# The last heads of a fused two-block transformer kernel: values between logits and masks, queries and keys transposed later, outputs split earlier

## The chip, the cores and the metric

The kernel runs on one NeuronCore of a Trainium2 chip. The metric is the device time of one execution in microseconds. TensorE (PE in the profile) does matmuls and transposes; VectorE (DVE), ScalarE (ACT) and GpSimd (POOL) do the elementwise work; SyncE (SP) issues the loads of weights. Each engine runs a program of its own in order, and the programs meet at semaphores.

## The reference

Two transformer blocks on a sequence of 256 tokens of width 1024, in float32. The first has two attention branches of 8 heads, a merge and a gated extra input. The second has two layers, each with a token mixer, a cross-attention of 4 heads to a memory of 256 entries, an output projection and an MLP. The change touches the second layer of the second block, whose mixer is this attention of 12 heads (with 256 tokens there is a single block of keys, so only the causal part is left):

```python
q, k, v = jnp.split(qkv, 3, axis=-1)
q = apply_rope(rms_norm(heads(q), q_gain), cos, sin)
k = apply_rope(rms_norm(heads(k), k_gain), cos, sin)
s_own = jnp.einsum('bhcd,bhkd->bhck', qc, k_own).astype(jnp.float32) * scale
s_own = jnp.where(kpos[None, :] <= qpos[:, None], s_own, NEG_2)
p = jax.nn.softmax(s, axis=-1).astype(v.dtype)
out = jnp.einsum('bhck,bhkd->bhcd', p_own, v_own)
...
x = x + jnp.concatenate([tok, mo], axis=-1) @ w_out[i]
u = rms_norm(x, g_mlp[i])
x = x + jnp.square(jax.nn.relu(u @ w_ff1[i])) @ w_ff2[i]
```

## The kernel before

**Dense products.** Activations (transposed, `a_hi`, `a_lo`, `b_hi`, `b_lo`) and weights are each split into a high and a low part, and a product is three matmuls, hi*hi, hi*lo and lo*hi. Weights come in units of 128 x 2048. SyncE loads a unit into `raw` (two places), ScalarE writes `w_hi` from it, VectorE `w_lo` (`unit(u)` on either engine splits unit u+3, into a ring of four), and TensorE multiplies: 24 matmuls of 128 x 512 a unit (`product`, L1796). SyncE may load unit u once `w_lo` of u-2 is made.

**Heads.** Heads are worked in pairs, by steps. Step n brings the logits of pair n, while the pair n-1 has its probabilities transposed and the pair n-2 is multiplied with its values. Between these small pieces TensorE runs a *fill*, a dense product that has nothing to do with the heads (`fill_of`, `one_fill`). There are three runs of steps; the change touches the last, `RUN3`, pairs 14 to 21 and steps 14 to 23. Pairs 14 and 15 are memory heads (their queries see all 256 keys, so their second half of keys has twice the width), 16 to 21 are the 12 causal heads. The fills of steps 14 to 19 are a whole unit each of the projection that makes the queries, keys and values of later pairs; those of steps 20 to 23 are a quarter of a unit each, six matmuls, of the output projection.

**The pieces of a step on TensorE**: `logits(n)`, `masks(n)` (adds the causal mask by a matmul with the identity and raises `s_ready`; memory heads have none), `qk_parts(n+1)` (transposes queries and keys of the next pair into the bank `b_io`), `values(n-2)` (raises `pv_done`), `transposes(n-1)` (the probabilities; the first half of the keys goes into bank `b_t`, the second into `b_io` too), and the fill. In `last_step`, a step n with n+1 in `LATE_PARTS` runs `qk_parts(n+1)` as a `mid` of its fill, before the third of four k-tiles; the others run it right behind the masks. Since both use `b_io`, an early `qk_parts(n+1)` comes before `transposes(n-1)`, which waits for its copy; a late one comes after, and waits until VectorE has copied the second half of pair n-1 (`pt_cp_v`).

**The others.** In step n ScalarE does `copy_qk(n+1)` (early, or late, behind `copy_pt`), for some steps squares of the next heads' rows (`SQUARES_AT`, used in steps 16 and 18), `exps(n, (0,))`, `out_hi(n-2)` (the high part of the pair's output, into `b_hi`), `exps(n, (1,))`, `copy_pt(n-1)`, the normalisation of the second head, the split of a unit, and an eviction of a block. VectorE does `maxima(n)` (two reductions and a small operation into `nmx` for each of the two heads), reductions of the squares, `copy_pt(n-1)`, the softmax factors and the normalisation of the first head, `out_lo(n-2)` (L1416), the split of a unit, an eviction. GpSimd rotates and scales queries and keys (`norm_and_rotate`) and raises `moba_made`, for which `qk_parts` waits.

`values(n)` waits for the low part of the pair before it, since both pairs' outputs use one bank:

```python
pe.wait_ge(pt_cp_a, pr + 1)
pe.wait_ge(pt_cp_v, pr + 1)
if pr:
    pe.wait_ge(pair_lo, pr)
```

and `logits(n)` waits for the exponentials of the step before: `pe.wait_ge(exp_done, 2 * (n - 1) + (1 if n % 2 == 0 and n > N_IDX else 2))`.

Of the kernel before, what the change touches and what calls it, by code (L numbers as in the profile page):

```python
# [84 lines left out]
RUN1, RUN2, RUN3 = range(0, 12), range(12, 14), range(14, 22)  # L85
# [71 lines left out]
BR_FILL = {12: 0, 13: 1}  # L157
DRAIN = (12, 13, 22, 23)
MOBA_FILL = {14 + i: i for i in range(6)}
LATE_PARTS = (16, 18, 20)  # L160
OUT_FILL = {20: 0, 21: 1, 22: 2, 23: 3}

SQUARES_AT = {15: (("k1", B_MOBA + 1), ("q2", B_MOBA + 1)), 17: (("k2", B_MOBA + 2),)}
# [26 lines left out]
def build(nc, a, out):  # L190
    with ExitStack() as ctx:
# [532 lines left out]
        def _(act):  # L724
# [14 lines left out]
            def unit(u):  # L739

                v = u + LOOK
                if v < N_UNITS:
                    split(v, v % RING, land_slot(v), unit_size(v))
# [101 lines left out]
            def last_step(n):  # L845

                if n + 1 in RUN3 and n + 1 not in LATE_PARTS:
                    copy_qk(n + 1)
                for squares_ in SQUARES_AT.get(n - 1, ()):
                    head_squares(*squares_)  # L850
                exps(n, (0,))
                if n - 2 in RUN3:
                    out_hi(n - 2)
                exps(n, (1,))
                if n - 1 in RUN3:
                    copy_pt(n - 1)
                if n + 1 in LATE_PARTS:
                    copy_qk(n + 1)
                if n - 1 in SQUARES_AT:
                    normalise_second(n)  # L860
                for u, k, half_, ks in fill_of(n):
                    if 3 in ks and u < U_MOBA + 7:
                        unit(u)
                if n - 1 not in SQUARES_AT:
                    normalise_second(n)
                for u, k, half_, ks in fill_of(n):
                    if half_ and 3 in ks:
                        block_done(u)
                        evac(k)
                late_unit(n)  # L870
# [27 lines left out]
            def exps(n, heads=range(2)):  # L898

                pr = n - N_IDX  # L900
                if pr >= 2:
                    act.wait_ge(pt_ready, pr - 1)
                else:
                    act.wait_ge(idx_acc, n - 1)
                for h in heads:
                    act.wait_ge(max_done, 2 * pr + h + 1)
                    for t in range(NT):
                        factor = SCALE if pr < N_GATES else query_factor(n, h)[:, t:t + 1]
                        logits = logits_of(n)[:, h, t, 0:width0(n) if t == 0 else S]
                        ins = act.activation(prob_of(n, t)[:, h, :], logits, ACT.Exp, scale=factor,  # L910
                                             bias=nmx[:, pr, t, h:h + 1], accum_out=psums[:, pr, t, h:h + 1])
                    ins.then_inc(exp_done, 1)
# [11 lines left out]
            def out_hi(n):  # L924

                pr = n - N_IDX
                if pr < N_GATES:
                    act.wait_ge(pair_tmp, pr + 1)
                    act.activation(b_hi[:, pair_ktile(pr), :], gated[:], ACT.Copy).then_inc(pair_hi, 1)
                    return  # L930
                act.wait_ge(pv_done, pr + 1)
                act.activation(b_hi[:, pair_ktile(pr), :], out_of(n), ACT.Copy).then_inc(pair_hi, 1)
# [262 lines left out]
        def _(dve):  # L1195
# [165 lines left out]
            def maxima(n):  # L1361

                pr = n - N_IDX
                for h in range(2):
                    dve.wait_ge(s_ready, 2 * n + h + 1)
                    if width0(n) == S:
                        link(dve.tensor_reduce(mx[:, pr, :, h], logits_of(n)[:, h], AX.X, ALU.max))
                    else:
                        dve.tensor_reduce(mx[:, pr, 0:1, h], logits_of(n)[:, h, 0, 0:P], AX.X, ALU.max).then_inc(*link.step())
                        link(dve.tensor_reduce(mx[:, pr, 1:2, h], logits_of(n)[:, h, 1, :], AX.X, ALU.max))  # L1370
                    if pr < N_GATES:
                        ins = dve.tensor_scalar(nmx[:, pr, :, h], mx[:, pr, :, h], -SCALE, None, ALU.mult)
                    else:
                        if kind_of(n)[:3] == "mem":
                            dve.wait_ge(memq_made, int(kind_of(n)[3]) + 1)
                        ins = dve.scalar_tensor_tensor(nmx[:, pr, :, h], mx[:, pr, :, h], -1.0, query_factor(n, h),
                                                       ALU.mult, ALU.mult)
                    ins.then_inc(max_done, 1)
# [28 lines left out]
            def out_lo(n):  # L1407

                pr = n - N_IDX
                kt = pair_ktile(pr)  # L1410
                dve.wait_ge(pair_hi, pr + 1)
                if pr < N_GATES:
                    dve.tensor_tensor(b_lo[:, kt, :], gated[:], b_hi[:, kt, :].bitcast(F32), ALU.subtract).then_inc(pair_lo, 1)
                    return
                dve.wait_ge(pv_done, pr + 1)
                dve.tensor_tensor(b_lo[:, kt, :], out_of(n), b_hi[:, kt, :].bitcast(F32), ALU.subtract).then_inc(pair_lo, 1)  # L1416
# [55 lines left out]
            def last_step(n):  # L1472

                maxima(n)
                for squares_ in SQUARES_AT.get(n - 1, ()) if n > RUN3[0] else (("q0", B_MOBA), ("q1", B_MOBA)):
                    head_squares(*squares_)
                if n - 1 in RUN3:
                    copy_pt(n - 1)
                if n - 1 not in SQUARES_AT:
                    if n + 1 == LATE_PARTS[1]:  # L1480
                        dve.wait_ge(moba_made, 2 * (HEADS[2 * (n + 1 - N_IDX)][1] // 4) + 2)
                    unit_before(n)
                if n > RUN3[0] and n - 1 not in SQUARES_AT:
                    factor_for_act(n)
                    normalise(n, (0,))
                else:
                    normalise(n, (0,))
                    factor_for_act(n)
                if n - 2 in RUN3:
                    out_lo(n - 2)  # L1490
                if n - 1 in SQUARES_AT:
                    unit_before(n)
                for u, k, half_, ks in fill_of(n):
                    if half_ and 3 in ks:
                        block_done(u)
                        evac(k)
# [285 lines left out]
        def _(pe):  # L1782
# [125 lines left out]
            def qk_parts(n):  # L1908

                if n:  # L1910
                    pe.wait_ge(qk_cp, n)
                copied = n - 2 if n in LATE_PARTS else n - 3
                if copied >= N_IDX:
# [34 lines left out]
            def logits(n):  # L1948

                kind, pr = kind_of(n), n - N_IDX  # L1950
                if n == RUN3[1]:
                    blocks_read(B_MOBA)
                pe.wait_ge(qk_cp, n + 1)
                if n and n != RUN2[-1]:

                    pe.wait_ge(exp_done, 2 * (n - 1) + (1 if n % 2 == 0 and n > N_IDX else 2))
                alone = kind[:3] in ("idx", "mem")
                keys = [(t, width0(n) if t == 0 else S) for t in range(NT)]
                for t, w in keys:
                    for h in range(2):  # L1960
                        rows = slice(HD * h, HD * h + HD)
                        ins = pe.matmul(logits_of(n)[:, h, t, 0:w], qk[rows, 0, t * P:t * P + P], k_of(n)[rows, 0:w],  # L1962
                                        start=alone or t == 0, stop=alone)
                        if alone and t == 1:
                            ins.then_inc(s_ready, 1)
# [25 lines left out]
            def transposes(n):  # L1991
# [14 lines left out]
                last = next(r[-1] for r in (RUN1, RUN2, RUN3) if n in r)  # L2006
                pe.wait_ge(qk_cp, min(n + (1 if n + 2 in LATE_PARTS else 2), last) + 1)
                for h in range(2):
# [78 lines left out]
            def last_step(n):  # L2087

                logits(n)
                masks(n)  # L2090
                late = n + 1 in LATE_PARTS
                if n + 1 in RUN3 and not late:
                    qk_parts(n + 1)
                (fill_,) = fill_of(n)
                if n - 2 in RUN3:
                    values(n - 2)
                    transposes(n - 1)
                    one_fill(fill_, {2: lambda: qk_parts(n + 1)} if late else ())
                elif n - 1 in RUN3:
                    one_fill(fill_, {2: lambda: transposes(n - 1), 3: lambda: qk_parts(n + 1)})  # L2100
                else:
                    one_fill(fill_)
# [226 lines left out]
```

## Time and profile before

| | us |
|---|---|
| time, median of 3 runs (lowest, highest) | 805.24 (805.05, 805.39) |
| the profiled execution: its time | 804.89 |
| the profiled execution: its span | 803.1 |
| TensorE busy in the span | 796.9 |
| VectorE, ScalarE, GpSimd busy | 529.9, 423.7, 110.0 |
| steps 14 to 23 of RUN3, about | 545.9 to 604.0 |

The span runs from the first to the last instruction; the time has 1.8 us more around it. In a timeline the first column is the start, the second the length, then the engine, the line of the code, the operation and its tiles, and how many were merged; in brackets the engine's idle time before it and what ended that. Ends of matmuls are modelled: each lasts longer in these rows than the distance to the next, so distances between starts are what counts on TensorE.

### The profile page before, as it was taken

To read this page: it belongs to the slowest core of one execution; us is meant where nothing else is said; L and a number is where in the kernel's file an instruction comes from. 1 tells how busy PE (TensorE), PEld (TensorE's weight loads), DVE (VectorE), ACT (ScalarE), POOL (GpSimd) and SP (SyncE) were. 2 spreads that over 40 slices of the span, in tenths; PEclk is the share of its full clock that TensorE was granted. 3 is DMA by queue.
4 is the path that set the end of the run, shared out by engine and by line. 5 is a ranking of instruction groups with operands and counts; after the bars stand their busy time and mean duration, and the time that the engine had idled before them with its cause. 6 is when DMAs were issued, how large, how long until landed. Compare 5 with 4: busy or idle time off the path is not lost.

```text
span 803.1 us, 11184 instructions
## 1 busy us (share of the span) xinstructions
PE 796.9 (99%) x4190; PEld 663.2 (83%) x4190; DVE 529.9 (66%) x708; ACT 423.7 (53%) x609; POOL 110.0 (14%) x143
## 2 busy tenths in 40 slices
PE   8999999999999999999999999999999999999998
PEld 7998988778888778888888888887777888888886
DVE  5647998677585767566656566578766756666561
ACT  5646556654755564364444435448774545434440
POOL 1610300000020510030000000068910000000000
PEclk9999999999999999999999999999999999999999
DMA  8961444356746633645655656461324466656541
GB/s 307 325 205 41 158 158 158 107 171 217 253 134 240 194 138 106 209 158 202 216 171 195 193 174 208 158 209 53 115 96 158 163 212 221 218 183 207 166 148 53
DMA packets 76743, 140.44 MB, mean 175 GB/s; under 512 B 2936, under 2 KB 23104, under 8 KB 76704
## 3 DMA queue, kind: packets, MB, share of 16 engines
q1 hardware_dynamic: 74608, 134.03, 50.0%
q0 software_dynamic: 1936, 5.82, 2.2%
q8 instruction: 25, 0.41, 0.2%
q14 instruction: 14, 0.11, 0.0%
q10 hardware_dynamic: 160, 0.07, 0.0%
HBM read 138.86 MB, written 1.05 MB: 174 GB/s over the span
## 4 chain that ended last, share of the span: by engine, by line
PE 97%; DVE 1%; ACT 1%; issue 0%; ACTq 0%; DVEq 0%
PE bank L1796 61%; PE bank L2182 13%; PE bank L2184 8%; PE bank L1962 2%; PE bank L1877 2%; PE bank L2186 2%; PE bank L2030 2%; PE bank L1828 1%; PE bank L1930 1%; PE bank L2004 1%; PE bank L1810 1%; PE bank L2010 1%; DVE w_lo L1216 1%; PE bank L2107 0%; PE bank L2229 0%; PE bank L1988 0%
## 5 line engine op out<-in xcount | busy, mean ns | idle before, releaser
L1796 PE MATMUL bank<-w_hi,a_both 128*128 128x512 f32 (+2 forms) x752 | 236.5, 384 | 0.2
L1216 DVE TENSOR_TENSOR w_lo<-raw,w_hi 128x2048 fp32r<-128x2048 f32 (+2 forms) x65 | 147.4, 2269 | 54.9 <-ACT w_hi L732 53.2
L1679 DVE TENSOR_TENSOR w_lo<-raw,w_hi 128x2048 fp32r<-128x2048 f32 x48 | 110.0, 2292 | 91.8 <-ACT w_hi L1118 91.0
L2182 PE MATMUL bank<-a_both,w_hi 128*128 128x512 f32 x448 | 161.4, 399 | 0.0
L1796 PEld LDWEIGHTS bank<-w_hi,a_both 128*128 128x128 f32 x752 | 140.7, 188 | 22.7 <-issue 2.0
L1118 ACT ACTIVATE w_hi<-raw 128x2048 fp32r<-128x2048 f32 x48 | 92.2, 1920 | 113.0 <-PE bank L1796 54.7
L732 ACT ACTIVATE w_hi<-raw 128x2048 fp32r<-128x2048 f32 (+1 forms) x63 | 119.3, 1893 | 59.2 <-PE bank L1796 34.4
L1796 PE MATMUL bank<-w_hi,b_hi 128*128 128x512 f32 x376 | 148.6, 395 | 0.1
L1796 PE MATMUL bank<-w_hi,b_lo 128*128 128x512 f32 x376 | 146.5, 390 | 0.0
L1796 PE MATMUL bank<-w_lo,b_hi 128*128 128x512 f32 x376 | 146.5, 390 | 0.0
L1796 PE MATMUL bank<-w_lo,a_both 128*128 128x512 f32 (+2 forms) x376 | 141.8, 377 | 0.0
L2184 PE MATMUL bank<-a_both,w_lo 128*128 128x256 f32 x512 | 133.0, 280 | 0.0
L2184 PEld LDWEIGHTS bank<-a_both,w_lo 128*128 128x128 f32 x512 | 96.6, 189 | 5.7
L2182 PEld LDWEIGHTS bank<-a_both,w_hi 128*128 128x128 f32 x448 | 84.3, 188 | 18.2
L1796 PEld LDWEIGHTS bank<-w_hi,b_lo 128*128 128x128 f32 x376 | 70.6, 188 | 15.1
L1796 PEld LDWEIGHTS bank<-w_hi,b_hi 128*128 128x128 f32 x376 | 70.6, 188 | 14.3 <-DVE b_lo L1663 0.5
L1796 PEld LDWEIGHTS bank<-w_lo,b_hi 128*128 128x128 f32 x376 | 70.7, 188 | 14.1
L1796 PEld LDWEIGHTS bank<-w_lo,a_both 128*128 128x128 f32 x376 | 70.8, 188 | 9.5
L574 POOL TENSOR_SCALAR stat<-stat 128x2 f32<-128x2 f32 x8 | 3.3, 410 | 305.8 <-ACT m L764 288.2
L1096 ACT ACTIVATE tok<-bank 128x256 f32<-128x256 f32 x64 | 23.5, 386 | 26.4 <-PE bank L2186 26.4
L1657 DVE TENSOR_TENSOR tok<-bank,tok 128x256 f32<-128x256 f32 x64 | 25.5, 421 | 6.8 <-ACT tok L1096 6.4
L1228 DVE SCALAR_TENSOR_TENSOR a_both<-bank,gain_cols,a_both 128x256 fp32r<-128x256 f32 x40 | 17.2, 480 | 14.6 <-ACT a_both L754 14.5
(248 smaller groups left out, 856.6 us busy)
## 6 DMA issues: line engine op xcount, KB each, us to landing
raw<-in_w_ff SPq DMA_DIRECT2D x64, 1024.0 KB, 5.1
raw<-in_w_in_moba SPq DMA_DIRECT2D x20, 512.0 KB, 4.3
raw<-in_w_merge SPq DMA_DIRECT2D x8, 1024.0 KB, 5.1
raw<-in_w_out SPq DMA_DIRECT2D x8, 1024.0 KB, 5.1
m<-in_w_in SPq DMA_DIRECT2D x6, 880.0 KB, 8.9
raw<-in_w_mem_kv SPq DMA_DIRECT2D x4, 1024.0 KB, 5.2
raw<-in_w_ple_gate SPq DMA_DIRECT2D x4, 1024.0 KB, 5.1
raw<-in_w_in_pool SPq DMA_DIRECT2D x4, 1024.0 KB, 5.1
```

Of the source, the lines that this page charges most:

```text
L732: act.activation(w_hi[:, slot, 0:n], landing[land][:, 0:n], ACT.Copy).then_inc(hi_ready, 1)
L1096: act.activation(hidden[:, f, :], b_hid[f][:, S:2 * S], ACT.Copy).then_inc(ff_part, 1)
L1118: act.activation(w_hi[:, (base + c) % RING, :], raw[:, (base + c) % RAW, :], ACT.Copy)\
L1216: dve.tensor_tensor(w_lo[:, v % RING, 0:n], landing[land_slot(v)][:, 0:n], w_hi[:, v % RING, 0:n].bitcast(F32), ALU.subtract).then_inc(lo_ ...
L1228: ins = dve.scalar_tensor_tensor(lo[:, k + q, :], ps[:, q * S:q * S + S], gain_cols[:, gain + k + q:gain + k + q + 1], hi[:, k + q, :].bit ...
L1657: dve.tensor_tensor(hidden[:, f, :], b_hid[f][:, 0:S], hidden[:, f, :], ALU.add).then_inc(ff_sum, 1)
L1679: dve.tensor_tensor(w_lo[:, (base + c) % RING, :], raw[:, (base + c) % RAW, :], w_hi[:, (base + c) % RING, :].bitcast(F32), ALU.subtract). ...
L1796: ins = pe.matmul(banks[t][:, 0:n], xa[:, kt, ts], wa[:, slot, w], start=first and k == 0 and q == 0, stop=last and k == kts - 1 and q == 2)
L1877: ins = pe.transpose(ps[:, kk * S + t * P:kk * S + t * P + P], src[:, t, (k + kk) * P:(k + kk) * P + P], ident[:])
L1962: ins = pe.matmul(logits_of(n)[:, h, t, 0:w], qk[rows, 0, t * P:t * P + P], k_of(n)[rows, 0:w], start=alone or t == 0, stop=alone)
L2182: pe.matmul(b_hid[f][:, :].rearrange("p (q n) -> p q n", q=2), w_hi[:, slot, w], both_, start=kt == 0, stop=False)
L2184: ins = pe.matmul(lo_, w_lo[:, slot, w], hi_, start=False, stop=False)
```

## The change

Three things, all in the steps of RUN3:
- TensorE: `values(n-2)` runs between `logits(n)` and `masks(n)`, except in the steps in which `qk_parts(n+1)` stays early.
- `LATE_PARTS` goes from 16, 18, 20 to all of 16 to 20. So `qk_parts` of pairs 17 and 19 moves from behind the masks of steps 16 and 18 to half of their fills, and ScalarE's `copy_qk` of these goes behind `copy_pt`. Only pair 21 keeps the early place, in step 20 (and pair 15 in step 14). The waits that depend on `LATE_PARTS`, in `qk_parts` and in `transposes`, follow.
- The outputs: ScalarE's `out_hi(n-2)` goes ahead of both heads' exponentials, VectorE's `out_lo(n-2)` to right behind `maxima(n)`.

`LATE_PARTS[2]` in VectorE's program is 18, as `LATE_PARTS[1]` was. In the diff the constant stands first, then `last_step` of ScalarE, of VectorE (with `maxima`) and of TensorE (with `logits`).

```diff
-LATE_PARTS = (16, 18, 20)
+LATE_PARTS = range(16, 21)
...
-                exps(n, (0,))
                 if n - 2 in RUN3:
                     out_hi(n - 2)
+                exps(n, (0,))
                 exps(n, (1,))
...
                 maxima(n)
+                if n - 2 in RUN3:
+                    out_lo(n - 2)
                 for squares_ in SQUARES_AT.get(n - 1, ()) if n > RUN3[0] else (("q0", B_MOBA), ("q1", B_MOBA)):
                     head_squares(*squares_)
                 if n - 1 in RUN3:
                     copy_pt(n - 1)
                 if n - 1 not in SQUARES_AT:
-                    if n + 1 == LATE_PARTS[1]:
+                    if n + 1 == LATE_PARTS[2]:
                         dve.wait_ge(moba_made, 2 * (HEADS[2 * (n + 1 - N_IDX)][1] // 4) + 2)
                     unit_before(n)
...
                     normalise(n, (0,))
                     factor_for_act(n)
-                if n - 2 in RUN3:
-                    out_lo(n - 2)
                 if n - 1 in SQUARES_AT:
                     unit_before(n)
...
                 logits(n)
+                late = n + 1 in LATE_PARTS
+                early = n + 1 in RUN3 and not late
+                if n - 2 in RUN3 and not early:
+                    values(n - 2)
                 masks(n)
-                late = n + 1 in LATE_PARTS
-                if n + 1 in RUN3 and not late:
+                if early:
                     qk_parts(n + 1)
                 (fill_,) = fill_of(n)
                 if n - 2 in RUN3:
-                    values(n - 2)
+                    if early:
+                        values(n - 2)
                     transposes(n - 1)
                     one_fill(fill_, {2: lambda: qk_parts(n + 1)} if late else ())
```

## Rows read from the trace of the kernel before

**Rows 1.** The page: busy time, share of the span and instructions, by engine.
```profile
PE 796.9 (99%) x4190; PEld 663.2 (83%) x4190; DVE 529.9 (66%) x708; ACT 423.7 (53%) x609; POOL 110.0 (14%) x143
```

**Rows 2.** Windows of steps 17, 18, 19: length, each engine's busy time, clock, DMA.
```profile
563.18:572.18 9.00, 9.00 (x56) 6.67 (x55) 7.44 (x14) 6.44 (x15) 8.64 (x6) 1.00 0.37 120
572.18:580.89 8.71, 8.71 (x56) 6.66 (x55) 7.30 (x15) 7.35 (x18) 8.12 (x8) 1.00 0.36 119
580.89:589.67 8.78, 8.78 (x55) 6.66 (x54) 6.04 (x13) 4.14 (x13) 3.96 (x5) 1.00 0.48 149
```

**Rows 3.** Timeline of TensorE, steps 20 to 23: values and logits.
```profile
591.30 0.87 PE L2030 MATMUL bank<-probT,proj 128*64 128x256 f32 x8
...
594.40 0.93 PE L1962 MATMUL bank<-qk 64*128 64x128 f32 x8
...
600.18 0.87 PE L2030 MATMUL bank<-probT,proj 128*64 128x256 f32 x8
...
603.18 0.87 PE L2030 MATMUL bank<-probT,proj 128*64 128x256 f32 x8
```

**Rows 4.** Timeline of VectorE, steps 21 and 22.
```profile
599.62 0.42 DVE L1416 TENSOR_TENSOR b_lo<-bank,b_hi 128x256 fp32r<-128x256 f32 x1
...
602.48 0.41 DVE L1429 COPY probT<-bank 128x256 f32<-128x256 f32 x1
```

**Rows 5.** Timeline of ScalarE, steps 20 and 21.
```profile
591.90 0.45 ACT L910 ACTIVATE prob<-bank,nmx,hstat 128x128 f32<-128x128 f32 x1
...
592.88 0.39 ACT L932 ACTIVATE b_hi<-bank 128x256 fp32r<-128x256 f32 x1
593.14 0.47 ACT L910 ACTIVATE prob<-bank,nmx,hstat 128x128 f32<-128x128 f32 x1
...
594.03 0.23 ACT L910 ACTIVATION_READ_ACCUMULATOR prob<-bank,nmx,hstat 128x1 f32 x1
...
599.91 1.93 ACT L732 ACTIVATE w_hi<-raw 128x2048 fp32r<-128x2048 f32 x1
```

**Rows 6.** Timeline of TensorE, RUN1: values, then the first mask matmul.
```profile
104.25 0.87 PE L2030 MATMUL bank<-probT,proj 128*64 128x256 f32 x8
105.06 0.23 PE L1983 MATMUL bank<-c_b,pick_b 128*128 128x128 bf16 x1
```

**Rows 7.** Timeline of ScalarE, step 16: the first exponential.
```profile
558.17 0.44 ACT L910 ACTIVATE prob<-bank,nmx,hstat 128x128 f32<-128x128 f32 x1
```

**Rows 8.** Timeline of VectorE, steps 16 to 18.
```profile
558.50 0.69 DVE L1283 TENSOR_REDUCE hstat<-m 128x8 f32<-128x512 f32 x1
...
559.99 0.68 DVE L1429 COPY probT<-bank 128x512 f32<-128x512 f32 x1
...
561.32 0.40 DVE L1416 TENSOR_TENSOR b_lo<-bank,b_hi 128x256 fp32r<-128x256 f32 x1
...
566.36 0.67 DVE L1376 SCALAR_TENSOR_TENSOR nmx<-mx,hstat 128x2 f32<-128x2 f32 x1
566.95 0.41 DVE L1429 COPY probT<-bank 128x256 f32<-128x256 f32 x1
...
575.99 0.41 DVE L1429 COPY probT<-bank 128x256 f32<-128x256 f32 x1
```

**Rows 9.** Timeline of TensorE: fills of steps 16 and 17, values(15), qk_parts(18).
```profile
557.53 0.47 PE L1796 MATMUL bank<-w_hi,a_both 128*128 128x512 f32 x1
...
564.37 1.08 PE L2030 MATMUL bank<-probT,memkv 128*64 128x256 f32 x8
...
566.01 0.49 PE L1796 MATMUL bank<-w_hi,a_both 128*128 128x512 f32 x1
...
568.88 0.60 PE L1930 MATMUL bank<-ident,proj 128*128 128x128 f32 x4
```

**Rows 10.** Timeline of GpSimd, steps 17 and 19.
```profile
565.73 1.28 POOL L665 TENSOR_TENSOR m<-m 128x512 f32<-128x512 f32 x1
...
584.26 0.74 POOL L673 TENSOR_TENSOR proj<-proj,m 128x256 f32<-128x256 f32 x1
```

## The prediction

> **What bounds the kernel now.** The page first: TensorE is busy 796.9 of 803.1 us [rows 1], and the chain of waits is nearly all its matmuls, so a microsecond of waiting or of extra matmul time that TensorE gets is a microsecond of the whole, and work of the others counts only where TensorE waits for it. Then the steps of the last heads, read from one `logits` to the next. They follow each other without idle time: the windows of steps 17, 18 and 19 have TensorE busy for their whole length [rows 2]. Step 18, which transposes queries and keys ahead of its fill, takes 8.71 us; step 19, which does it at half of the fill, takes 8.78 [rows 2]. With less fill to cover the exponentials, the only waits of some size come near the end. `values(20)` starts at 600.18 [rows 3], 0.14 us after VectorE's `out_lo(19)` ends at 600.04 [rows 4]; `values(21)` at 603.18 [rows 3] follows its fill without a wait, and by that pattern 0.20 us is lost at `values(20)`. `logits(21)` at 594.40 [rows 3] comes 0.14 after the last accumulator read of `exps(20)` (594.03 + 0.23) [rows 5], some 0.1 late. I take 0.14 us as the time from another engine's end to TensorE's start. So waits of 0.3 us are all that is to be had in this stage.
>
> **Values between logits and masks.** No instruction is added. RUN1 has this order already: `values` at 104.25, first mask matmul at 105.06 [rows 6], 0.81 us for eight matmuls and no gap; so the order itself costs nothing. What it does is to give `pv_done(n-2)` earlier and `s_ready(n)` 0.80 us later. In steps 16 to 19 a fill of over 5 us lies between the exponentials and their next reader, and covers that.
>
> **Outputs split ahead.** ScalarE's `out_hi(n-2)` moves ahead of `exps(n)`, VectorE's `out_lo(n-2)` ahead of the squares, of `copy_pt(n-1)` and of the softmax. Again nothing is added, but both are in-order programs here: `out_lo` needs `out_hi`, and all that stands behind it waits.
>
> **Queries and keys at half of the fill, steps 16 and 18.** Late `qk_parts(17)` must wait for `copy_pt(15)`, since both use the bank `b_io`: `qk_parts` asks for `pt_cp_v` of n-2 where n is late, of n-3 where it is not. Step 16 is the step in which VectorE is behind. Worked out:
> - ScalarE is through the two squares at 558.17 [rows 7] and now does `out_hi(14)` there, 0.39 us as in the row of its kind [rows 5]: 558.56.
> - VectorE is through its maxima at 558.50 [rows 8] and now starts `out_lo(14)` at 558.58. An `out_lo` is 0.40 us long (561.32) and holds it for some 0.33 before the next can start [rows 8], so the two reductions of squares start at 558.91 and not at 558.50, +0.41. From the first of them to `copy_pt(15)` are 1.49 us (558.50 to 559.99), and the copy takes 0.68 because the heads before have two halves of keys [rows 8]. End: 558.91 + 1.49 + 0.68 = 561.08; TensorE may go at 561.22.
> - TensorE reaches half of the fill 2.87 us after its start (566.01 to 568.88 in step 17) [rows 9]. Step 16's fill started at 557.53 with `qk_parts(17)` ahead of it [rows 9] and starts earlier without: it is there by 560.4 at the latest, and waits 0.8 us or more.
> - From `qk_parts` at half to the next `logits` are 3.30 us (568.88 [rows 9] to 572.18 [rows 2]): `logits(17)` at 561.22 + 3.30 = 564.52, where it stands at 563.18 now [rows 2]. **+1.34 us.** What TensorE saves or waits earlier in the step doesn't enter, as VectorE sets this.
> - Bounds: with `out_lo` free and no latency the copy ends at 560.67, and the step ends at 563.97: +0.79. With another 0.3 of delay on VectorE +1.65. I take 1.34.
>
> Behind it, step 17: `copy_pt(16)` (566.95 + 0.41 = 567.36) [rows 8] comes later by the 1.34, by `values(15)` ahead of the masks, at most 1.08 (564.37) [rows 9], and by `out_lo`, 0.33: 570.11 at the latest. `qk_parts(18)` wants to start at 568.88 + 1.34 = 570.22 and may at 570.25: hidden, or as good as. Step 18: `copy_pt(17)` (575.99 + 0.41) [rows 8] comes 1.34 + 0.80 + 0.33 later, 578.87, so TensorE may go at 579.01. It gets there 2.62 us (`logits` to fill, the 2.83 from 563.18 to 566.01 less 0.21, as its `values` take 0.87 and not 1.08) and 2.87 us after `logits(18)` at 573.52: 579.01. Hidden, with nothing to spare. So step 18 costs just the difference of the forms, 8.78 - 8.71 = **+0.07** (0 to 0.4). GpSimd's last rotation is done at 585.00 [rows 10], and `qk_parts(20)` wants it after 587; its queue gets nothing new, and starts its later heads 0.4 to 1.4 us later. No DMA is added; the loads of the last weights wait for `w_lo`, some 0.8 us later, with a fill of margin.
>
> What VectorE's two small `nmx` operations take depends on GpSimd: one took 0.67 us (566.36 to 567.03) [rows 8] and ended as GpSimd's 1.28 us instruction from 565.73 did [rows 10]. The Trainium skill (SBUF — State Buffer, "SBUF: two separate sides") says that the two share a pair of ports under an exclusive lock, held for the whole instruction. By that rule the trace agrees, and an `nmx` that meets the start of such an instruction is held for all of it; the sums above keep the holds as they fell in this trace, and a rival below takes them longer.
>
> **Steps 20 to 22.** Step 20 is early, with `values(18)` behind masks and `qk_parts(21)`: it ends at 591.30 + 0.87 = 592.17 [rows 3], and ScalarE now wants it ahead of `exps(20)`, which started at 591.90 [rows 5]. The block from there to 594.26 holds the same instructions, and starts at 592.21: +0.31, and `logits(21)` goes at 594.71. From there masks come after `values(19)`, 0.80 later: +1.11 for the maxima of step 21. ScalarE gets 0.26 back, as `out_hi(19)` has left the middle of `exps(21)` (592.88 to 593.14 in step 20) [rows 5]: +0.85 for the rest of its queue, in which stand `copy_pt(20)`, the second normalisation, a weight split of 1.93 us [rows 5], `out_hi(20)`. Behind `out_hi(20)` are VectorE's `out_lo(20)` and `copy_pt(21)`, which ended at 602.90 [rows 4]: 603.75, and `values(21)` goes at 603.89 and not 603.18 [rows 3]. TensorE itself would be there at 603.18 + 0.31 - 0.20 = 603.29. So the 0.20 is gained, and a wait of 0.6 put in its place. **+0.71** (0.2 to 1.0: lowest if `exps(20)` doesn't slip and a third of the chain has slack, highest if `copy_pt(20)` too delays `values(20)`).
>
> Behind these steps the chain of waits is matmuls up to the last addition, so nothing takes it back. Sum: 1.34 + 0.07 + 0.71 = 2.12 us. The profiled execution took 804.89 us around a span of 803.1, 0.35 under the median of 805.24; on the median 807.36, said **807.3**.
>
> **The rivals.**
> - *As said, and so not slower.* The two waits that the change aims at go, and `qk_parts` costs its 0.07 each: 805.24 - 0.30 + 0.14 = 805.1. It needs `copy_pt(15)` by 560.2, which ran to 560.67 even before. 0.06.
> - *Only the end pays.* If VectorE is less behind in step 16 in most executions than in the profiled one, the loss there is no more than 0.4: 805.24 + 0.4 + 0.07 + 0.7 = 806.4. For it: one execution; against: VectorE stands idle there for no more than 0.20 us between two of its own reductions, so its queue sets the time by itself. 0.20.
> - *Faster.* Were transposes in the middle of a fill free, TensorE would get back two times 0.60 (568.88) [rows 9] and the 0.30 of waits: 803.7, still inside the 0.2% named below; and the longer window of step 19 against 18 [rows 2] shows them not free. 0.02.
> - *Ports collide.* The masks come at another point of GpSimd's work; each `nmx` held 0.6 us longer than now in steps 17 and 18 makes `qk_parts(18)` and `(19)` wait, 1.2 us together: 808.6. The 0.6 is a whole 1.28 in place of the 0.67 [rows 8, 10]. For it: nothing to spare in step 18; against: holds of before may as well go. 0.12. It is what the lock in the Trainium skill (SBUF — State Buffer, "SBUF: two separate sides") would do at its worst.
> - *The forecast*, 0.60: 806.6 to 807.9.
>
> **How the numbers follow.** A measurement of this kernel tells some 0.2% (1.6 us) from no change; slower begins at 806.85. Slower: 0.60 less 0.05 for its low end, 0.12, and 0.01 of the second case: 0.68. Faster 0.02, same 0.30. The range 805.5 to 808.3 leaves out the first and third rival (805.1 and 803.7), part of the fourth and the lowest of the second.
>
> **What would show it.** In the profile after: a gap of TensorE of about 1 us in the middle of step 16's fill, released by VectorE's `copy_pt` (probT, 128x512); `logits(17)` 1.3 us later than before; steps 17 and 19 of the same length; `logits(21)` just behind `exps(20)`; no wait at `values(20)` for `b_lo`, but one at `values(21)` for VectorE's probT copy. It is wrong if step 16 has no gap, or if TensorE's dense stretches change pace.

## The result and the profile after

| | before | changed |
|---|---|---|
| time, median of 8 runs each (lowest, highest), us | 805.0 (804.86, 805.39) | 807.43 (806.92, 807.71) |
| ratio to before, 95% interval | | 1.0029 (1.0020 to 1.0039) |
| the profiled execution: its time, its span, us | 804.89, 803.1 | 807.44, 805.6 |

The change makes the kernel 2.4 us slower, more than the 0.2% that can be told; 807.3 had been forecast. The figure is nearer than the sum behind it: 2.1 us had been added to a median of 805.24, and 2.4 were measured on one of 805.00, so that the lower base hides most of the 0.3 us by which the sum is short. The question left is whether the kernel is slower for the reasons given. (One execution each of experiments 6 and 7 below took 989.64 and 1599.59 us and stands apart from all others; without them the medians given there are 806.58 and 806.41.)

First what TensorE waits for in the stage (view of waits, 545 to 640 us, changed kernel; columns: engine, tile, line, what ended the wait, then us in all, times, longest). The same view of the kernel before is empty.

```profile
PE bank L1930 <- issue: 1.2, 1, 1.2
PE bank L2030 <- DVE probT L1429: 0.5, 1, 0.5
PE bank L1962 <- ACT prob L910: 0.3, 1, 0.3
PE bank L2030 <- issue: 0.2, 1, 0.2
PE bank L2004 <- DVE tok L1388: 0.2, 1, 0.2
```

The same waits in their places (TensorE's timeline, changed kernel; the next to last is values(20), the last values(21)):

```profile
554.29 0.93 PE L1962 MATMUL bank<-qk 64*128 64x128 f32 x8
...
556.73 0.66 PE L2004 MATMUL bank<-ident,tok 128*128 128x128 f32 x4 [0.17 <-DVE tok L1388]
...
561.84 0.63 PE L1930 MATMUL bank<-ident,proj 128*128 128x128 f32 x4 [1.24 <-issue]
...
565.13 0.93 PE L1962 MATMUL bank<-qk 64*128 64x128 f32 x8
...
575.04 0.87 PE L2030 MATMUL bank<-probT,proj 128*64 128x256 f32 x8
...
591.41 0.93 PE L1962 MATMUL bank<-qk 64*128 64x128 f32 x8
...
596.46 0.93 PE L1962 MATMUL bank<-qk 64*128 64x128 f32 x8 [0.35 <-ACT prob L910]
...
602.13 0.87 PE L2030 MATMUL bank<-probT,proj 128*64 128x256 f32 x8 [0.18 <-issue]
...
605.72 0.87 PE L2030 MATMUL bank<-probT,proj 128*64 128x256 f32 x8 [0.54 <-DVE probT L1429]
```

And the windows of steps 17, 18 and 19 (columns as in [rows 2]):

```profile
565.13:574.00 8.87, 8.87 (x56) 6.63 (x55) 7.60 (x14) 6.47 (x15) 8.36 (x7) 1.00 0.43 129
574.00:582.77 8.77, 8.65 (x56) 6.63 (x55) 6.38 (x15) 7.20 (x18) 6.02 (x6) 1.00 0.31 111
582.77:591.41 8.64, 8.64 (x55) 6.63 (x54) 5.03 (x13) 4.81 (x14) 3.98 (x5) 1.00 0.49 146
```

Read against the kernel before, from one `logits` to the next (before, step 16 ran from 554.04 to 563.18):

| stretch | before | changed | difference | forecast |
|---|---|---|---|---|
| step 16 | 9.14 | 10.84 | +1.70 | +1.34 |
| step 17 | 9.00 | 8.87 | -0.13 | 0 |
| step 18 | 8.71 | 8.77 | +0.06 | +0.07 |
| step 19 | 8.78 | 8.64 | -0.14 | 0 |
| logits(20) to logits(21) | 4.73 | 5.05 | +0.32 | +0.31 |
| logits(21) to values(21) | 8.78 | 9.26 | +0.48 | +0.40 |
| sum | | | +2.29 | +2.12 |

The span has grown by 2.5 us. The missing 0.25 is there already when step 16 begins (554.29 for 554.04), ahead of everything that the change touches. In the kernels below logits(16) starts between 553.97 and 554.41 (but at 555.44 in experiment 6), and none of them changes anything ahead of it, so this is the scatter of single executions. Times of the changed kernel up to step 16 are read with that offset.

The wait at 561.84 carries the name "issue" and no releaser. It is the awaited one all the same: VectorE's second-half copy ends at 561.05 + 0.68 = 561.73 in its timeline, 0.11 us before. Step 16 on VectorE and GpSimd in the changed kernel:

```profile
558.87 0.42 DVE L1416 TENSOR_TENSOR b_lo<-bank,b_hi 128x256 fp32r<-128x256 f32 x1
559.22 0.68 DVE L1283 TENSOR_REDUCE hstat<-m 128x8 f32<-128x512 f32 x1
560.45 0.69 DVE L1283 TENSOR_REDUCE hstat<-m 128x8 f32<-128x512 f32 x1 [0.56 <-DVE hstat L1283]
561.05 0.68 DVE L1429 COPY probT<-bank 128x512 f32<-128x512 f32 x1
...
561.85 1.34 DVE L1388 TENSOR_SCALAR prob<-prob,prec 128x128 f32<-128x128 f32 x2
561.99 1.05 POOL L663 TENSOR_TENSOR m<-proj,hstat 128x512 f32<-128x512 f32 x1
...
563.18 3.37 DVE L1216 TENSOR_TENSOR w_lo<-raw,w_hi 128x2048 fp32r<-128x2048 f32 x1
```

### The profile page after: what moved, and what is told of

Its sections match the earlier page's. It is cut to its first block, busy times and chain, and to the rows that moved or that the text cites. A ratio compares the mean times of both kernels' runs of the same rounds, so it can differ in the third digit from the quotient of the medians.

```text
span 805.6 us, 11184 instructions
## 1 busy us (share of the span) xinstructions
PE 796.0 (99%) x4190; PEld 662.5 (82%) x4190; DVE 529.7 (66%) x708; ACT 424.1 (53%) x609; POOL 108.7 (13%) x143
## 3 DMA queue, kind: packets, MB, share of 16 engines
HBM read 138.86 MB, written 1.05 MB: 174 GB/s over the span
## 4 chain that ended last, share of the span: by engine, by line
PE 94%; DVE 3%; ACT 1%; DMA 1%; issue 1%; SPq 0%; ACTq 0%
PE bank L1796 61%; PE bank L2186 13%; PE bank L2188 7%; PE bank L1962 2%; PE bank L2190 2%; PE bank L1877 2%; PE bank L2030 1%; DVE w_lo L1216 1%; PE bank L1930 1%; DMA raw<-in_w_in 1%; PE bank L2004 1%; PE bank L1810 1%; PE bank L2010 1%; ACT w_hi L732 0%; PE bank L2233 0%
```

## The experiments

All were timed in five rounds against the kernel before on the same chip, 10 to 12 executions each (experiment 5 only 5). The first three do one part of the change each. The lengths of steps are those of one profiled execution.

**1. Only queries and keys at half of the fill** (kernel before, one part).

```diff
-LATE_PARTS = (16, 18, 20)
+LATE_PARTS = range(16, 21)
```

> The kernel before with LATE_PARTS = range(16, 21) alone; values and outputs stay where they were. Theory of the wait (transposes of pair 17 at half of step 16's fill wait for VectorE's copy of pair 15): a gap in the middle of step 16's fill, but shorter than in the changed kernel, as no output split stands ahead of that copy; logits(17) about 0.9 us later than before, step 18 0.07 longer, end steps as before: 806.0 us (+1.0). Rival (the loss is in the order of the last steps alone): no gap, +0.1, 805.1 us.

Measured: 805.88 against 804.91, ratio 1.0012 (1.0003 to 1.0021). Step 16 takes 10.03 us, +0.89, with TensorE idle for 0.50 at `qk_parts(17)`; step 18 takes 8.75, +0.04; all the rest is as before to 0.01. So this part alone is a loss, and in the place named.

**2. Only values between logits and masks.**

```diff
 logits(n)
+if n - 2 in RUN3 and not early:
+    values(n - 2)
 masks(n)
```

> The kernel before with values(n-2) between logits and masks in steps 17, 19 and 21 alone. By the trace of the changed kernel the order masks, transposes saves 0.14 us in each of steps 17 and 19; in step 21 the maxima come 0.8 us later, and the low part of pair 19, which stays behind the softmax, with them, so values(20) waits about 0.8 us longer: -0.28 + 0.8 = +0.5, 805.5 us. Rival (the end steps have slack for it): -0.3, 804.7 us.

Measured: 805.90 against 804.91, ratio 1.0012 (1.0003 to 1.0021). That is 0.99 us and not the 0.5 expected. The waits for `b_lo` are there, 1.07 us at values(20), since `out_lo(19)` comes later behind the later maxima, and 0.25 at values(19), which had not been expected: `out_lo(18)` is wanted sooner and comes no sooner. Steps 17 and 19 are shorter, 8.85 and 8.64. Step 19 shows where, in distances between starts. The kernel before:

```profile
581.74 0.40 PE L1988 MATMUL bank<-mask_b,ident_b 128*128 128x128 bf16 x4
582.07 0.87 PE L2030 MATMUL bank<-probT,proj 128*64 128x256 f32 x8
582.87 0.66 PE L2004 MATMUL bank<-ident,prob 128*128 128x128 f32 x4
583.37 0.38 PE L2010 MATMUL bank<-ident,prob 128*128 128x128 f32 x2
```

The changed kernel, with the order of experiment 2:

```profile
583.62 0.87 PE L2030 MATMUL bank<-probT,proj 128*64 128x256 f32 x8
584.43 0.40 PE L1988 MATMUL bank<-mask_b,ident_b 128*128 128x128 bf16 x4
584.66 0.61 PE L2004 MATMUL bank<-ident,prob 128*128 128x128 f32 x4
585.11 0.38 PE L2010 MATMUL bank<-ident,prob 128*128 128x128 f32 x2
```

The four mask matmuls hold TensorE 0.33 us when values follow and 0.23 when transposes do; the transposes take 0.50 behind values and 0.45 behind masks; values take 0.80 or 0.81 either way. That is 0.14 us for the pair of orders, and the 0.14 of the table.

**3. Only the outputs ahead** (`out_hi` and `out_lo` as changed; nothing on TensorE).

```diff
+if n - 2 in RUN3:
+    out_hi(n - 2)
 exps(n, (0,))
-if n - 2 in RUN3:
-    out_hi(n - 2)
...
 maxima(n)
+if n - 2 in RUN3:
+    out_lo(n - 2)
```

> The kernel before with both output splits moved ahead alone. Exponentials of step 20 wait for values(18): logits(21) 0.3 us later; the wait of values(20) for the low part of pair 19 (0.2 us) goes; values(21) waits a little for the copy of its probabilities: +0.15, 805.15 us, no gap in step 16. Rival (splitting ahead is what costs in step 16 too, by VectorE's queue): a gap in step 16 and +1 us or more.

Measured: 806.82 against 804.91, ratio 1.0027 (1.0017 to 1.0036). This is a clear miss: 1.7 us above what I expected, and not by the rival either, as step 16 has no gap and takes 9.13 us. The ten executions lie far apart, from 805.80 to 809.19 (the kernel before: 804.54 to 805.46); the profiled one took 806.90. Step 17 takes 9.21 and step 18 9.53 us, 0.2 and 0.8 more than before, and TensorE waits 0.77 us at values(16) for ScalarE's eviction. The chain that ended there, followed back (pieces of the chain, 555 to 580 us, outputs only; start, length, what):

```profile
560.78 0.60 DVE probT L1429
...
561.48 1.34 DVE prob L1388 x2
562.89 3.29 DVE w_lo L1216
...
566.21 0.37 SPq L496
...
566.62 4.92 DMA raw<-in_w_out
...
574.10 0.65 ACT proj L786
574.79 0.87 PE bank L2030 x8
```

VectorE's `out_lo(14)` pushes its two small normalisations to where they run into GpSimd's 1.05 us instruction (1.34 us for both and not 0.55), so `w_lo` starts 1.2 us later and ends 1.55 later (566.18 for 564.63), SyncE may load the next unit only then, the load of 4.92 us reaches ScalarE at 571.5 when it should split it, and ScalarE's eviction of the block, queued behind that split, is what values(16) waits for: they read that block. The rest of the loss: logits(21) waits 0.35 for the exponentials, as in the changed kernel, and 0.75 us is lost after step 23, 0.46 of it in one wait at 669.07 for VectorE's `b_lo` in the MLP, where ScalarE waits 35.0 us for weight loads and not 20.0. That the late loads cause this last part is argued, not shown; no other kernel here loses anything there, and the changed kernel, with 29.3 us of such waits, doesn't either.

**4. The changed kernel with `qk_parts(17)` early again.** The diff is to the changed kernel.

```diff
-LATE_PARTS = range(16, 21)
+LATE_PARTS = (16, 18, 19, 20)
```

> The changed kernel with pair 17's queries and keys transposed early again (LATE_PARTS = 16, 18, 19, 20). Theory of the wait: the gap in step 16 goes and 1.7 of the 2.3 us with it: 805.6 us. Rival (the last steps carry the loss): 807.3 us or a little under.

Measured: 806.97 against 804.91, ratio 1.0026 (1.0016 to 1.0035). The wait of step 16 is gone (logits(16) to logits(17) 9.14 us), and in the profiled execution all of its 1.7 us comes back behind it: steps 17 and 18 take 9.26 and 10.08. So the 805.6 expected was missed by 1.4 us. The median lies near the rival ("the last steps carry the loss", 807.3), but the trace has the loss in steps 17 and 18 and not in the last ones. The medians leave some 0.4 us gained, which the two intervals can't tell from nothing. TensorE's timeline, qk_parts(18) and values(16):

```profile
569.04 0.63 PE L1930 MATMUL bank<-ident,proj 128*128 128x128 f32 x4 [0.23 <-POOLq L676]
...
574.73 0.87 PE L2030 MATMUL bank<-probT,proj 128*64 128x256 f32 x8 [1.43 <-ACT proj L786]
```

So two chains grow out of `out_lo(14)` in VectorE's queue: a short one to `qk_parts(17)`, and a long one through `w_lo`, the load and the eviction to values(16). In the changed kernel the wait of the short one gives the long one time, and nothing of the long one is left. ScalarE's timeline has the eviction that values(16) wait for, first in the kernel before, then in the changed one:

```profile
572.50 0.68 ACT L786 ACTIVATE proj<-bank,stat 128x512 f32<-128x512 f32 x1
```

```profile
574.32 0.67 ACT L786 ACTIVATE proj<-bank,stat 128x512 f32<-128x512 f32 x1
```

It ends 1.00 us behind logits(18) before and 0.99 in the changed kernel, but 2.42 and 2.31 in experiments 3 and 4. There is still a small wait at values(16) in the changed kernel: they start 1.04 behind logits(18), and not the 0.85 of step 19. These 0.19 us come from the new place of values, which are now wanted before that eviction ends. Experiments 6, 7 and 12 have 1.04 or 1.05 too, though their `w_lo` ends at other times.

**5 and 6. `out_lo(14)` back at its old place**, in the kernel of experiment 3 and in the changed kernel.

```diff
 maxima(n)
-if n - 2 in RUN3:
+if n - 2 in RUN3 and n != 16:
     out_lo(n - 2)
...
     factor_for_act(n)
+if n == 16:
+    out_lo(n - 2)
```

> outputs_only, but in step 16 VectorE's out_lo(14) stays behind the softmax, where it was. Theory of the weights: out_lo(14) ahead makes VectorE's high-part subtraction for the weights late, the load behind it late, ScalarE's split and eviction of step 17 late, and values(16) waits for that eviction; with out_lo(14) back the 0.8 us wait at values(16) and the longer step 17 go, and only the last steps' +0.2 is left: 805.1 us. Rival (ScalarE's order, out_hi ahead of the exponentials, is what costs): as outputs_only, 806.8 us.

> The changed kernel, but in step 16 VectorE's out_lo(14) stays behind the softmax. Theory of the prediction: the copy of pair 15 comes 0.4 us earlier (0.7 with the longer pause between the two reductions, if that pause comes from the order), the gap at half of step 16's fill shrinks from 1.24 to about 0.5, logits(17) 0.7 earlier: 806.7 us. Rival (the gap is set by something else, such as the transposes' own place): 807.4 us.

Measured, 5: 807.61 against 804.98, ratio 1.0034 (1.0021 to 1.0047), and so no faster than with `out_lo(14)` ahead, where 805.1 had been expected. Steps 16 to 18 are again as before (logits(19) at 580.86), so the long chain is indeed rooted in this one instruction. But a new wait of 2.21 us stands at `qk_parts(20)`. Timeline of the profiled execution (809.15 us, the slowest of its runs), VectorE, GpSimd and the TensorE row:

```profile
577.47 2.27 DVE L1216 TENSOR_TENSOR w_lo<-raw,w_hi 128x2048 fp32r<-128x2048 f32 x1
577.62 3.64 POOL L640 TENSOR_TENSOR hstat<-hstat,half 128x8 f32<-128x8 f32 x1
...
585.58 2.35 DVE L1216 TENSOR_TENSOR w_lo<-raw,w_hi 128x2048 fp32r<-128x2048 f32 x1
585.75 2.77 POOL L673 TENSOR_TENSOR proj<-proj,m 128x256 f32<-128x256 f32 x1
...
588.71 1.09 PE L1932 MATMUL bank<-ident,proj 128*128 128x128 f32 x4 [2.21 <-POOLq L676]
```

Twice `w_lo` starts 0.15 to 0.17 us ahead of a GpSimd instruction, and twice the latter ends only after it: 3.64 us, and 2.77 where [rows 10] has 0.74 for the same instruction. This is the lock that the prediction weighed. The Trainium skill (SBUF — State Buffer, "SBUF: two separate sides") gives the shared ports to whichever of the two starts first, for its whole instruction. With VectorE first the trace agrees; with GpSimd first it does so only in part, as experiment 10 shows.

Step 19 takes 12.77 us here, 3.99 more than before, and only 2.37 of these lie ahead of `qk_parts(20)`. From there to the next logits TensorE takes 4.92 us where it takes 3.30 otherwise. The windows show why (the third figure from the end is the granted clock, as a part of 2.4 GHz):

```profile
580.86:588.71 7.85, 5.64 (x39) 4.04 (x39) 6.57 (x13) 3.06 (x10) 7.42 (x6) 1.00 0.37 133
588.71:591.73 3.02, 3.02 (x9) 2.54 (x10) 0.15 (x1) 1.28 (x3) 0.00 (x0) 0.50 0.86 253
592.37:593.63 1.26, 1.26 (x7) 0.76 (x5) 0.00 (x0) 0.00 (x0) 0.00 (x0) 1.00 0.07 24
```

Behind the wait of 2.21 us the granted clock is 0.50, that is 1.2 GHz, for some 3 us, and this costs another 1.6 us. Of the five executions this one and the next slowest (808.94) have a mean clock of 0.998, as has the slowest of experiment 3 (809.19); the other three of experiment 5 (807.23 to 807.61) have one of 1.000. So the median has the wait but, as it seems, not the slow clock.

Measured, 6: 806.61 against 804.98, ratio 1.0019 (1.0011 to 1.0028), as expected: the wait at `qk_parts(17)` is 0.47 us, step 16 takes 10.14. (The profiled execution took 807.75; 1.15 us more than in the changed kernel had gone by before step 16.)

**7. The copy ahead of everything in step 16** (changed kernel; `copy_pt(15)` directly behind `maxima(16)`).

```diff
 maxima(n)
+if n == 16:
+    copy_pt(n - 1)
 if n - 2 in RUN3:
     out_lo(n - 2)
```

> The changed kernel, but in step 16 VectorE copies pair 15's probabilities first, ahead of out_lo(14) and the two reductions. Both theories: the gap in the middle of step 16's fill goes. If that wait is all that is lost there, step 16 costs 0.07 more than before: 805.9 us. Theory of the weights (a second chain behind the same VectorE queue ends nearly as late): values(16) waits 1 us or more for ScalarE's eviction, as in early_in_16, and the time stays near that: 806.9 us.

Measured: 806.48 against 804.98, ratio 1.0018 (1.0009 to 1.0027). `qk_parts(17)` starts at 560.29 without a wait and step 16 takes 9.44 us; 0.26 is lost at `qk_parts(18)`, for GpSimd, whose factors now start behind copy and `out_lo` (560.27, for 559.27 before). Step 17 takes 9.29 us for that, and step 18 takes 8.93, as `qk_parts(19)` comes 0.10 behind VectorE's copy (577.97 + 0.41). In step 16 there are 0.3 us more than before although nothing waits in the fill: the transposes start 0.58 us behind the masks (556.02 to 556.60) and not 0.23, as they wait for VectorE's normalisation. The same wait stands at 556.73 in the changed kernel, where the later one covers it. The sum of all steps is +1.48 us: this is the 0.6 by which the median lies above the simpler of the two expectations. The other one, a wait of 1 us or more at values(16), was wrong: `w_lo` runs here from 562.07 to 564.34 with GpSimd's instruction behind it and not ahead, and values(16) lose no more than the 0.2 us of the changed kernel.

**8. Only what pays**: kernel before, values first in steps 16, 17 and 19, and `out_lo(19)` behind the maxima of step 21.

```diff
 logits(n)
+if n in (16, 17, 19):
+    values(n - 2)
 masks(n)
...
 maxima(n)
+if n == 21:
+    out_lo(n - 2)
```

> The kernel before with only the parts that the traces show to gain: values between logits and masks in steps 16, 17 and 19 (0.14 us each in 17 and 19, 0.1 in 16), and in step 21 VectorE's out_lo(19) right behind the maxima (0.2 us wait at values(20), of which 0.15 is left at values(21)). LATE_PARTS and ScalarE as before. Expected -0.5: 804.4 us; rival (these are taken back at the next wait): 804.9 us.

Measured: 804.91 against 804.98, ratio 0.9999 (0.9990 to 1.0008), so the rival was right and not the 804.4 expected. Steps 17 and 19 give their 0.14 each, but step 16 takes 9.44: `qk_parts(17)` starts later behind values, so do ScalarE's copy and the transposes that wait for it (0.25 at L2012).

**9. Only steps 20 and 21 as changed**, on the kernel before.

```diff
-if n - 2 in RUN3:
+if n >= 20:
     out_hi(n - 2)      # out_lo(n - 2) likewise
...
+if n == 21:
+    values(n - 2)
 masks(n)
```

> The kernel before with the change in steps 20 and 21 alone (out_hi and out_lo ahead in both, values(19) between logits and masks in step 21). The prediction's term for these steps by itself: logits(21) 0.31 us later behind the exponentials of step 20, the wait at values(20) for the low part gone, a wait at values(21) of 0.6, steps 16 to 19 as before: +0.7, 805.65 us. Rival (this term is bound up with the lateness from step 16): within 0.3 of before.

Measured: 805.80 against 805.04, ratio 1.0009 (1.0000 to 1.0018). The distances are those of the changed kernel to 0.01 us: 5.04, 5.68 and 3.59 from logits(20) over logits(21) and values(20) to values(21), with the same idle times of 0.35, 0.19 and 0.54. The loss at the end is a thing of its own, +0.80 in the trace; by the times alone, with an interval down to 1.0000, it is only just told.

**10. The outputs ahead only from step 19 on** (as experiment 5, with `out_lo` ahead for n >= 19 only, and so back in its old place in steps 17 and 18 as well).

```diff
 maxima(n)
-if n - 2 in RUN3:
+if n >= 19:
     out_lo(n - 2)
```

> outputs_only, but VectorE's out_lo is ahead only in steps 19 to 21. In outputs_lo_late_16 VectorE's subtraction for the weights of step 18 began 0.15 us before a GpSimd instruction, not 0.3 after it, GpSimd stood still for it, and qk_parts(20) waited 2.2 us for GpSimd. Theory of the order of arrival: with out_lo(16) back ahead of that subtraction GpSimd is first again, step 19 has its 8.78 us, no wait for GpSimd: 805.1 us. Rival (ScalarE's order is what makes GpSimd late): the wait stays, 807 us.

Measured: 805.23 against 805.04, ratio 1.0003 (0.9994 to 1.0012). Without `out_lo` ahead in steps 17 and 18, GpSimd comes first and both go through, as VectorE's and GpSimd's timelines show:

```profile
577.83 1.66 POOL L640 TENSOR_TENSOR hstat<-hstat,half 128x8 f32<-128x8 f32 x1
578.09 2.28 DVE L1216 TENSOR_TENSOR w_lo<-raw,w_hi 128x2048 fp32r<-128x2048 f32 x1
```

Step 19 is 8.78 us long again. ScalarE's order, the rival, is the same in both kernels, so it was the collision that cost experiment 5 its 2.2 us. By the rule quoted there `w_lo` would be held until GpSimd's instruction ends at 579.49; but it takes 2.28 us, no more than by itself. So the first comer was not seen to hold the other for its whole length in this pair.

**11. As experiment 8, without step 16.**

```diff
-if n in (16, 17, 19):
+if n in (17, 19):
     values(n - 2)
```

> picked without its step 16 (values(14) behind the masks again, so that qk_parts(17) and its copy aren't late for the transposes of pair 15, which cost 0.25 us). Values between logits and masks in steps 17 and 19 alone save 0.14 us each, and out_lo(19) ahead moves 0.2 us of wait from values(20) to values(21): -0.3, 804.7 us. Rival: nothing, 805.0 us.

Measured: 804.58 (804.39 to 805.53) against 805.04, ratio 0.9998 (0.9989 to 1.0007). TensorE waits for nothing in the stage. Its timeline has logits(21), values(20) and values(21):

```profile
594.12 0.93 PE L1964 MATMUL bank<-qk 64*128 64x128 f32 x8
...
599.69 0.87 PE L2032 MATMUL bank<-probT,proj 128*64 128x256 f32 x8
...
602.85 0.87 PE L2032 MATMUL bank<-probT,proj 128*64 128x256 f32 x8
```

logits(21) comes 0.28 us earlier than before [rows 3], the two times 0.14. values(20) gets the 0.21 that was forecast as gained, and values(21) gives back 0.16 of it (3.16 behind values(20) for 3.00). This is the fastest version; by its interval it can't be told from the kernel before, and so neither expectation is ruled out.

**12. `out_lo(14)` behind the reductions, ahead of the copy** (changed kernel). This is about the 0.56 us in the VectorE rows above: before, the second reduction starts 0.20 us after the first.

```diff
 maxima(n)
-if n - 2 in RUN3:
+if n - 2 in RUN3 and n != 16:
     out_lo(n - 2)
 for squares_ in ...: head_squares(*squares_)
+if n == 16:
+    out_lo(n - 2)
```

> The changed kernel, but in step 16 VectorE's out_lo(14) stands between the two reductions of the squares and copy_pt(15), where the change has it ahead of both. Everything else is as changed. In the changed kernel the second reduction starts 0.56 us after the first has ended, where it is 0.20 us in the kernel before. Theory: the longer pause comes from out_lo standing directly ahead of the first reduction. Then the pause is 0.20 here, out_lo still costs its 0.33, and copy_pt(15) starts 0.43 us earlier (0.36 of the pause and 0.07 of the step from nmx to the next instruction): the wait of qk_parts(17) is 0.8 us and not 1.24, step 16 takes 10.4 us and not 10.84, and the time is 807.0. Rival: the pause comes from something else that the change has moved in this step (ScalarE's or TensorE's new order), and out_lo is innocent of it: the pause stays 0.56, the wait 1.2, the step 10.8 and the time 807.4. The pause in the profile decides, as 0.4 us is less than the timing can tell.

Measured: 806.96 against 805.39, ratio 1.0020 (1.0011 to 1.0029). Timeline of VectorE, with the TensorE row:

```profile
558.59 0.69 DVE L1283 TENSOR_REDUCE hstat<-m 128x8 f32<-128x512 f32 x1
...
559.48 0.69 DVE L1283 TENSOR_REDUCE hstat<-m 128x8 f32<-128x512 f32 x1 [0.20 <-DVE hstat L1283]
...
560.41 0.68 DVE L1429 COPY probT<-bank 128x512 f32<-128x512 f32 x1
...
561.20 0.63 PE L1932 MATMUL bank<-ident,proj 128*128 128x128 f32 x4 [0.80 <-issue]
```

The pause is 0.20 again, the wait 0.80 and step 16 takes 10.43 us, each as the theory had it. In all, four kernels have 0.56 (the changed one, experiments 3, 4 and 7) and ten have 0.20. Experiment 7, in which the copy stands ahead of `out_lo` and `out_lo` still directly ahead of the reductions, has the 0.56. So the longer pause goes with `out_lo` directly ahead. What in the engine makes it stays open; the second reduction waits for the first's semaphore in all of them.

## Why the prediction was right, point by point

**The place and the mechanism of step 16: right. Its size: too small by 0.36.** The term was 1.34 and measured 1.70. The runs take it apart, by the length of step 16: 0.89 for the late place alone (experiment 1), 0.11 for the order of the others on top (10.03 to 10.14, experiments 1 and 6), 0.29 for `out_lo`'s hold (10.14 to 10.43, experiments 6 and 12), and 0.41 for its place ahead of the reductions (10.43 to 10.84, experiment 12 and the changed kernel), 0.36 of it their longer pause. The prediction took "From the first of them to `copy_pt(15)` are 1.49 us" over from the kernel before; there it is 1.49, and behind `out_lo` 1.83 (559.22 to 561.05). That distance was not a property of the two instructions. The measured 1.70 lies just above the bounds of 0.79 to 1.65, and the upper one had come near only by "another 0.3 of delay" that nothing was named for.

**"So the order itself costs nothing": wrong.** It gains 0.14 us in a step, twice. [rows 6] show values ahead of masks, but only one of the transitions; what follows the masks changes too, and that row was not looked for. In step 16 the same order costs 0.30 if `qk_parts` stays early (experiment 8). These gains of 0.28 and the 0.36 missing in step 16 cancel in good part, and so the sum, +2.29 for +2.12, is nearer than its terms.

**Steps 17 to 19: the hidden copies were hidden**, with no wait at `qk_parts(18)` (570.68) or `qk_parts(19)` (579.50). The difference of the forms is 0.04 and not 0.07 (experiment 1). Missed was a wait of 0.19 at values(16): the list of what values wait for had probabilities and the pair's output in it, but not the eviction of the block that they read (`blocks_read` in `values`), and values(16) are the first to read a block of a fill of these steps. That eviction ends some 1.0 us behind logits(18), before as after; values came 1.63 behind them before, and in the new order could come 0.85 behind. Order and wait nearly cancel there, which is why +0.07 looks exact at +0.06.

**"The loads of the last weights wait for `w_lo`, some 0.8 us later, with a fill of margin": wrong in the margin.** With the outputs alone `w_lo` starts 1.2 us later, and from its end to values(16) there is less than no margin: it costs 0.77 us at values(16) (experiment 3). In the changed kernel the wait of step 16 covers it whole. Right by cover, not by reasoning; experiment 4 took the cover away and lost 1.43 us there.

**Steps 20 to 22: right.** logits(21) was forecast at 594.71 and comes, with the 1.74 us by which logits(20) is later taken off, at 594.72; values(21) were forecast at 603.89 and come at 603.98, since TensorE starts 0.26 us behind VectorE's copy there (605.46 to 605.72) and not 0.14. +0.80 for +0.71. That `copy_pt(20)` delays values(20), named as the case for the upper end, happens with 0.18 us, and so the "0.20 gained" there is not to be seen. In experiment 11 it is, and it is given back behind values(21) all but 0.05.

**The rivals.** The changed kernel bears out neither "as said", nor "only the end pays" (step 16 lost its 1.7 in the profiled execution, and the medians agree). The ports did collide, in VectorE's normalisation and `w_lo` of step 16 (1.34 and 3.37 us), but the price did not come as 1.2 us at `qk_parts(18)` and `(19)`. Experiment 5 had the full price in one place, 2.2 us, from an order of arrival 0.15 us wide. The 0.12 given to that rival concerned a real hazard. The trace before has GpSimd's instruction 0.29 us ahead of `w_lo` (577.45 and 577.74); on which side it would fall after a change the prediction did not ask.

## What to carry to other kernels

When a late piece is moved later still to share a bank, look for the copy that frees the bank and count everything queued ahead of it on its engine, in the one step where that engine is behind; moving it is only free where the other engines have slack. A distance between two instructions read in one order isn't carried over to another: read the pair of neighbours that the change makes, and all inputs of the instruction that moves ahead (its bank, its sources, the eviction that writes them). And a loss that is covered by another one has to be named as such, since undoing the first brings out the second, as experiment 4 did. And a piece put back can move two other instructions past each other, as in experiment 5.

## What the runs showed of the hardware

- A few tenths of a microsecond decide which of VectorE and GpSimd is held: GpSimd's 128x8 instruction took 1.66 us when it began 0.26 ahead of `w_lo` (2.28 us, not held), and 3.64 when it began 0.15 behind.
- Behind a wait of 2.21 us TensorE's granted clock was 0.50 for some 3 us (experiment 5), and the stretch to the next logits took 4.92 us and not 3.30. Behind the waits of 1.24 us (changed kernel) and 1.43 us (experiment 4) it stayed at 1.00.
- Two reductions of 128x512, the second waiting for the first, have 0.20 us between them in ten kernels, and 0.56 in the four in which a subtraction that reads the bank stands directly ahead of them. The cause is open.
- The 4 mask, 8 values and 6 transpose matmuls of a step cost TensorE 0.14 us less in the order values, masks, transposes than in the order masks, values, transposes, for the same instructions.
- The same wait costs TensorE different distances: it starts 0.11 us behind VectorE's copy at `qk_parts(17)`, 0.20 behind ScalarE's at values(20) (601.93 to 602.13) and 0.26 behind VectorE's at values(21), where 0.14 had been taken for all.
